# Pooling input and recurrent values as one product with 512 moving columns at a part's start

## The reference

```
proj = h @ w_in[l]
(u_pool, z_ssd, xbc_ssd, dt_ssd, q_h, f_h, i_h, g_h, q_mem, gate_logits) = jnp.split(proj, split_at, axis=-1)
branches = (pool_mixer(u_pool, ...), ssd_mixer(z_ssd, xbc_ssd, dt_ssd, ...),
            hgrn2_mixer(q_h, f_h, i_h, g_h, ...), memory_attention(q_mem, mem, w_mem_kv[l]))
merged = sum over n of sigmoid(gate_logits)[n] * (branches[n] @ w_branch[l, n])
h = layer_norm(ALPHA * h + merged @ w_o[l], ...)
h = layer_norm(ALPHA * h + moe_ffn(h, ...), ...)
```

## Time and profile before

| | |
|---|---|
| median of 3 runs | 2230.35 us (2230.19 to 2231.26) |
| the profiled execution, its own time | 2230.57 us |
| its span | 2228.8 us |
| PE matmuls busy | 2190.8 us, 98% |
| DVE busy | 1180.9 us, 53% |
| ACT busy | 700.2 us, 31% |

### The profile page before, as it was taken

The page is one execution under the profiler, slowest core; times in us unless marked ns, Lnnn a source line. Parts: engine busy times, 40 slices in busy tenths (PEclk is TensorE's granted clock), DMA queues, the critical chain, the costliest instruction groups (busy, mean ns, idle before and its releaser), DMA issues.

```text
span 2228.8 us, 29982 instructions
## 1 busy us (share of the span) xinstructions
PE 2190.8 (98%) x11648; PEld 1535.4 (69%) x11648; DVE 1180.9 (53%) x1495; ACT 700.2 (31%) x778; POOL 12.4 (1%) x28
## 2 busy tenths in 40 slices
PE   8999999999999999999999999999999999999996
PEld 7889899898888888888888944444444444444442
DVE  6457786777765545444557733443333444433435
ACT  4443434444353333344343311111111111111112
POOL 1000000000000000000000000000000000000000
PEclk9999999999999999999999999999999999999998
DMA  7444444444455555555656599999999999999996
GB/s 287 170 176 155 161 151 162 151 162 151 156 185 196 192 195 188 188 193 192 236 209 236 227 383 427 427 427 428 428 428 428 428 428 429 428 429 429 428 427 276
DMA packets 62174, 635.28 MB, mean 285 GB/s; under 512 B 7424, under 2 KB 7552, under 8 KB 10384
## 3 DMA queue, kind: packets, MB, share of 16 engines
q1 hardware_dynamic: 60192, 627.30, 71.1%
q0 software_dynamic: 752, 4.75, 0.6%
q10 hardware_dynamic: 1152, 2.10, 0.3%
HBM read 632.02 MB, written 2.10 MB: 285 GB/s over the span
## 4 chain that ended last, share of the span: by engine, by line
PE 75%; DMA 18%; DVE 5%; issue 1%; ACT 1%; SPq 0%; DVEq 0%; ACTq 0%
PE bank L328 28%; DMA wgu<-wgu 17%; PE bank L893 13%; PE bank L296 8%; PE bank L941 5%; PE bank L281 5%; PE bank L298 4%; PE bank L558 3%; PE bank L841 3%; PE bank L851 3%; DVE wlo L1286 1%; DVE fr L1498 1%; DMA wdt_raw<-wdt 1%; PE bank L874 0%; DMA raw<-units 0%
## 5 line engine op out<-in xcount | busy, mean ns | idle before, releaser
L1286 DVE TENSOR_TENSOR wlo<-raw,whi 128x2048 fp32r<-128x2048 f32 x185 | 423.9, 2291 | 344.7 <-ACT whi L989 344.1
L989 ACT ACTIVATE whi<-raw 128x2048 fp32r<-128x2048 f32 x185 | 354.1, 1914 | 421.6 <-PE bank L328 344.4
L893 PE MATMUL bank<-wgu,xg 128*64 128x512 f32 x2048 | 448.8, 593 | 3.9 <-DMA wgu<-wgu 3.9
L893 PEld LDWEIGHTS bank<-wgu,xg 128*64 128x64 f32 x2048 | 145.5, 137 | 300.4 <-issue 281.9
L296 PE MATMUL bank<-x_split,whi 128*128 128x512 f32 x896 | 319.8, 400 | 0.8 <-DVE wlo L1286 0.8
L328 PE MATMUL bank<-whi,x_split 128*128 128x512 f32 x1024 | 319.6, 390 | 0.0
L298 PE MATMUL bank<-x_split,wlo 128*128 128x256 f32 x896 | 251.1, 280 | 0.0
L941 PE MATMUL bank<-wd,eactT 128*64 128x512 f32 x1024 | 226.8, 596 | 0.0
L328 PEld LDWEIGHTS bank<-whi,x_split 128*128 128x128 f32 x1024 | 192.2, 188 | 39.9
L1832 DVE SCALAR_TENSOR_TENSOR eact<-eth,bank 128x256 f32<-128x256 f32 x32 | 13.5, 422 | 364.6 <-issue 192.7
L328 PE MATMUL bank<-wlo,x_split 128*128 128x512 f32 x512 | 199.4, 389 | 0.0
(11 more groups left out here) (378 smaller groups left out, 2869.2 us busy)
## 6 DMA issues: line engine op xcount, KB each, us to landing
wgu<-wgu SPq DMA_DIRECT2D x128, 2048.0 KB, 21.6
raw<-units SPq DMA_DIRECT2D x204, 1024.0 KB, 4.9
wd<-wd SPq DMA_DIRECT2D x64, 2048.0 KB, 18.7
raw<-units SPq DMA_DIRECT2D x6, 512.0 KB, 6.9
stage<-units SPq DMA_DIRECT2D x2, 1024.0 KB, 13.0
h<-xtok POOLq DMA_DIRECT2D x2, 1024.0 KB, 9.1
out<-acc SPq DMA_DIRECT2D x3, 512.0 KB, 2.6
stage<-units SPq DMA_DIRECT2D x2, 512.0 KB, 9.3
```

What stands on the lines that cost most here:

```text
L893: mi = nc.tensor.matmul(bank[3][CAP * j:CAP * j + CAP, :], buf[:, 4 * c + k, CAP * (2 * half + j):CAP * (2 * half + j + 1)], wgu_t[c][:, j ...
L989: nc.scalar.activation(whi[u % SPLIT][:, :], raw[u % RAW][:, :], ACT.Copy).then_inc(hi_done, 1)
L1286: V.tensor_tensor(wlo[u % SPLIT][:, :], raw[u % RAW][:, :], whi[u % SPLIT][:, :].bitcast(f32), ALU.subtract).then_inc(lo_done, 1)
```

## The change

The inputs POOL and VAL become one, PV, of four units with 4 x 128 rows of 512 columns (256 of pooling, 256 of values), multiplied by `dense_wide` into banks 0 and 1: the left half of each bank is the pooling input, the right half the values. It stands behind QMEM at a part's start, so that PE's program of a part begins with the third and fourth unit of PV, and ends with QMEM and the first two units of PV of the next part. The order is QMEM, PV (4), FGT, QRY, XS, BC, OGATE, ZG. The number of units of a part stays 18. ACT copies the values right behind the pooling input. In the last part the last four places are the first four units of the merge, which goes on with its fifth. HALF_BANK, the banks of the memory values and of the merge change with it.

As unit numbers of the steps from FGT to OGATE rise by two, so do the u at which ACT and DVE do them (5 becomes 7, and so on; ZG stays at 18). The reciprocal of rh and its two products, which stood at u = 21 and 22, are made functions `root_out` and `head_out` and stand at u = 5 and 6 of the next part's loop, behind the last part on their own. The first masks stay at the start of a part's loop, one step later than the join of QMEM.

```diff
-HALVES = 9
-QMEM, POOL, FGT, QRY, XS, BC, OGATE, VAL, ZG = range(HALVES)
-UP = 2 * HALVES
+QMEM, PV, FGT, QRY, XS, BC, OGATE, ZG, NEXT_QMEM, NEXT_PV = range(10)
+FIRST_UNIT = (0, 2, 6, 8, 10, 12, 14, 16, 18, 20)
+UP = 18
...
-HALF_BANK = {QMEM: 0, FGT: 2, QRY: 0, XS: 2, BC: 0, OGATE: 2, ZG: 2, HALVES: 0}
+HALF_BANK = {QMEM: 2, FGT: 2, QRY: 0, XS: 2, BC: 0, OGATE: 2, ZG: 0, NEXT_QMEM: 2}
...
+        for j in range(2):
+            dense_wide(pe, N_P0 + 2 + j, N_P0 + 2 + j, bank[0:2], xhi, xlo, WK * j, j == 0, False)
...
-                n = N_P0 + 2 * h + j
+                n = N_P0 + FIRST_UNIT[h] + j
                 if j == 0:
 
-                    if h == POOL:
-                        pe.wait_ge(s["y1_ok"], p + START)
-                    elif h == VAL:
-                        pe.wait_ge(s["dec_ok"], 3 * p + 3)
-                    elif (h, p) != (FGT, 0):
-                        pe.wait_ge(s["join_ok"], joins(p, {FGT: QMEM, QRY: QMEM, XS: FGT, BC: QRY, OGATE: XS,
-                                                           ZG: OGATE, HALVES: BC}[h]) - (h == FGT))
-                if h == HALVES and last_part:
-                    if j == 0:
+                    if h == QRY:
+                        pe.wait_ge(s["u_ok"], p + 1)
                         pe.wait_ge(s["vh_ok"], p + 1 + START)
-                    dense_wide(pe, p * UP + n, n, bank[0:2], xhi, xlo, WK * j, j == 0, False)
-                elif h in (POOL, VAL):
-                    dense(pe, p * UP + n, n, bank[5], xhi, xlo, UK * j, j == 0, j == 1, True)
+                    else:
+                        pe.wait_ge(s["join_ok"], joins(p, {FGT: QMEM, XS: FGT, BC: QRY, OGATE: XS, ZG: BC,
+                                                           NEXT_QMEM: OGATE, NEXT_PV: ZG}[h]))
+                if h in (NEXT_QMEM, NEXT_PV) and last_part:
+                    i = 2 * (h - NEXT_QMEM) + j
+                    dense_wide(pe, p * UP + n, n, bank[2:4], xhi, xlo, WK * i, i == 0, i == 3)
+                elif h in (PV, NEXT_PV):
+                    dense_wide(pe, p * UP + n, n, bank[0:2], xhi, xlo, WK * j, j == 0, j == 3)
                 else:
...
-            half(1, 0)
-            half(1, 1)
-            half(2, 0)
+            half(PV, 2)
+            half(PV, 3)
+            half(FGT, 0)
...
-            half(7, 0)
+            half(ZG, 0)
             level(6)
-            half(7, 1)
+            half(ZG, 1)
...
-            half(8, 0)
+            half(NEXT_QMEM, 0)
             level(8)
-            half(8, 1)
-            half(HALVES, 0)
+            half(NEXT_QMEM, 1)
+            half(NEXT_PV, 0)
 
...
-                if u == 4:
-                    act.wait_ge(unit_used, half_count(p, 2))
+                if u == 6:
+                    act.wait_ge(unit_used, half_count(p, PV + 1))
                     act.wait_ge(s["dp_ps"], p + START)
-                    nc.scalar.activation(upool[:, :, :], b3(5), ACT.Copy).then_inc(s["u_ok"], 1)
-                if u == 5:
+                    nc.scalar.activation(upool[:, :, :], banks[:, 0:2, 0:UC], ACT.Copy).then_inc(s["u_ok"], 1)
+                    act.wait_ge(s["o_ps"], p + START)
+                    nc.scalar.activation(vh[:, :, :], banks[:, 0:2, UC:2 * UC], ACT.Copy).then_inc(s["vh_ok"], 1)
+                if u == 7:
                     act.wait_ge(s["dp_ps"], p + 1 + START)
                     act.wait_ge(s["yp_ps"], p + START)
                     nc.scalar.activation(dpool[:, :, :], b3(7), ACT.Copy).then_inc(s["dp_ok"], 1)
-                if u == 7:
+                if u == 9:
                     act.wait_ge(s["join_ok"], joins(p, FGT))
...
-                if u == 16:
-                    act.wait_ge(unit_used, half_count(p, 8))
-                    act.wait_ge(s["o_ps"], p + START)
-                    nc.scalar.activation(vh[:, :, :], b3(5), ACT.Copy).then_inc(s["vh_ok"], 1)
...
+            def root_out(q):
+
+                dve.wait_ge(s["osd_ok"], q + 1)
+                step(V.reciprocal(rh, rh))
+
+            def head_out(q):
+
+                step(V.scalar_tensor_tensor(rh, bank[6][:, :], hnw[:, 0:1], rh, ALU.mult, ALU.mult))
+                V.scalar_tensor_tensor(yT[:, 2, bass.ts(q, 2), :], rh.rearrange("p (a b) -> p a b", a=2), 0.5,
+                                       gs[:, :, :], ALU.mult, ALU.mult).then_inc(s["yh_ok"], 1)
...
                     joined(qm[:, :, :], QMEM)
+                if u == 5:
                     dve.wait_ge(s["dec_ps"], 3 * p + START)
                     masks(0)
-                if u == 5:
+                    if p > 0:
+                        root_out(p - 1)
+                if u == 6 and p > 0:
+                    head_out(p - 1)
+                if u == 7:
                     masks(1)
                     if p > 0:
                         state_out(p - 1)
                     dve.wait_ge(s["ys_ok"], 2 * p + START)
...
-                if u == 21:
-
-                    dve.wait_ge(s["osd_ok"], p + 1)
-                    step(V.reciprocal(rh, rh))
-                if u == 22:
-                    step(V.scalar_tensor_tensor(rh, bank[6][:, :], hnw[:, 0:1], rh, ALU.mult, ALU.mult))
-                    V.scalar_tensor_tensor(yT[:, 2, bass.ts(p, 2), :], rh.rearrange("p (a b) -> p a b", a=2), 0.5,
-                                           gs[:, :, :], ALU.mult, ALU.mult).then_inc(s["yh_ok"], 1)
 
             if p == PARTS - 1:
+                root_out(p)
+                head_out(p)
                 state_out(p)
 
         for p in range(PARTS):
```

## The result

The changed kernel takes 2248.16 us (median of 4 runs, 2247.59 to 2248.89), the kernel before 2230.81 us in the same runs: a ratio of 1.0075 [1.0063, 1.0087], **17.4 us slower**. The forecast was 2243.9 in a range of 2238 to 2249, so sign and range held. The time lies 0.2 us above the 2248 to which the forecast's own case went, the clock's 1.5 us included. The sum in it was +13.5, and 3.9 us are missing from it. The profiled execution took 2248.89 us.

The account below looks back on a forecast made before the run. TensorE was taken to bound the parts, so its waits there arrive in full. Boundaries between parts +12.9, last boundary +5.3, wider product -4.7 gave +13.5 us: 2243.9 us, range 2238.0 to 2249.0.

Parts of the forecast that it names:

- the forecast's own case: Waits at all four boundaries, width gain as in the rows: 2239.8 to 2246.4, to 2248 with the clock; chance 0.78.
- the clock's 1.5 us: Extra time if the clock falls in the last boundary's 5.3 us wait, giving 2245.4.
- The bound, TensorE's waits for low halves: In the parts only TensorE's stay moves the end; what is gained or lost there arrives in full.
- The wait at place 1: Second unit after the sums of squares: TensorE waits 3.0 us, as ScalarE's loop head precedes its high half.
- The wait at place 2: Forget gate's first unit: another 1.3 us, as VectorE's masks and reciprocal stand ahead of its low half.
- Seven waits with some 18 us: Expected profile of TensorE's waits for low halves: three of 3.0, three of 1.3, one of 5.3 us.
- The three boundaries together: Boundaries between parts: 4.3 us each by both waits, 12.9 us in all, bounds 9.9 to 14.4.
- The last boundary: Behind the last part: VectorE's reciprocals and products precede place 1's low half; 5.3 us wait (5.0 to 5.6).
- The rival with a falling clock: Clock falls in waits: 1.5 us at the last, up to 6 with all; many waits or no width gain: 0.09.
- The gain from the width: 16 pooling and value units with 512 instead of 256 columns: 0.295 us each, 4.7 us gained (4.0 to 5.5).
- The faster rival: No boundary waits because low halves keep ahead; place 1's high half must start by 242.2: 2225.7 us; chance 0.06.
- Only the last boundary waits: Rival: ScalarE's head falls in idle time and the masks fit, leaving +5.3 - 4.7: 2231.0 us; chance 0.07.

Follow-up runs that it names:

- e1_half_first: Changed kernel with ScalarE's high half for place 1 ahead of its loop's head and VectorE's join of qm behind that unit's low half: 2239.71 us.
- e3_last: Changed kernel with the norms' last steps behind the last part spread over the merge, and ScalarE's first branch copy one step later: 2240.88 us.
- e2_masks: Changed kernel with VectorE's first two masks behind the head products instead of ahead of the reciprocal: median 2248.46 us, profiled execution 2243.71.
- e5_fill: Changed kernel with matmuls nobody reads in TensorE's waits, 12 at each boundary between parts and 20 at the last: 2245.04 us.
- e8_qm_at_head: e4_all with qm's copy and join back at the start of the part: 2228.87 us, ratio 0.9992 to the kernel before.
- e7_all_narrow: e4_all with each 512-column PV matmul made as two of 256: 2231.8 us, ratio 1.0006 to the kernel before.
- e4_all: Changed kernel with the edits of e1_half_first, e2_masks and e3_last together, and qm copied and joined in the part before: 2227.62 us, ratio 0.9984.
- e4_again: The same kernel as e4_all, measured once more beside the kernel before: 2227.24 us, ratio 0.9985.
- e6_narrow: Changed kernel with each 512-column PV matmul made as two of 256 columns: 2250.73 us, ratio 1.0087 to the kernel before.
- after_again: The changed kernel unaltered, measured once more beside e5_fill and others on one chip: 2247.63 us, ratio 1.0073.

## Why the prediction was right, and where the sum was off

- **The bound, TensorE's waits for low halves: right.** The waits that e1_half_first and e3_last took away arrived at the end in full, and a little more; what e2_masks took away did only where the clock held.
- **The wait at place 1, 3.0 forecast: right in cause, half a microsecond short in size.** The list has 3.1, 3.0 and 3.1, but it counts from the end of the last matmul of place 0; counted as the forecast did, from a place 0 of 5.46 us, it is 3.5, 3.4 and 3.4. What made it was shown by e1_half_first. The way from the second root to the high half took 3.8 us and was 3.2 in the sum: the second DMA issue took 0.95 us (0.90 and 0.95 at the next two boundaries) where the earlier trace rows had 0.39. At the third boundary of the kernel before the same issue takes 0.86, so one boundary was read where three stood in the trace. Place 0 to place 1 thus takes 8.92 us where the sum had 8.46.
- **The wait at place 2, 1.3 forecast: right in cause, hidden in the result.** It stands as 1.15 where the clock held (third boundary, e5_fill) and was covered where it fell. "Seven waits with some 18 us" was therefore not what the profile showed: five over a microsecond, with 14.0 + 1.15 = 15.2 us. That VectorE's order makes it is shown by e2_masks and e8_qm_at_head.
- **The three boundaries together: 12.9 forecast, 14.3 measured**, as 16.13 + 15.85 + 15.79 less 3 x 11.15. Nearly all of the 1.4 is the longer head. From the forecast's own 2 x 5.46 it is 15.0, above its upper bound of 14.4.
- **The last boundary: 5.3 forecast, 7.1 measured.** The wait, from the cause given, was 4.8 in the list and 5.2 counted as the forecast did; it cost 4.3, because it took in the wait of 0.4 that the kernel before had at place 3, and the slow clock added 2.7. Here the step failed that kept the clock out of the sum "because no wait inside the trace is long enough to tell". The rival with a falling clock priced it at 1.5 us here, and it is what happened, in both profiled executions of the changed kernel. How much it takes differs from one execution to the next: the 552 matmuls from place 1 on take 128.19 and 127.59 us in the two profiles of the changed kernel, 126.80 in e1_half_first and 127.01 in e2_masks, and 125.41 in e5_fill, whose clock held. That rival's other half, some 4.5 of its 6 us for the three waits of 3.0, did not come: the clock fell at two of three boundaries and cost little there, because the slow matmuls covered the second wait. That the terms overlap was not seen in the prediction, which added them. That the total stayed within the range is owed to the room left for that rival.
- **The gain from the width: 4.7 forecast, 4.2 to 4.9 measured** (e7_all_narrow against e4_all). The Trainium skill, TensorE: Matmul & The Clock Gate, Back-to-back issue gap, would have 1.0 us here by its formula N / 2.4 + 2.5 ns; the runs speak against it, with 0.28 to 0.30 us a unit for its 0.06.
- **The gain seen without the waits is only 3.4 to 3.6** (e4_all, e4_again against before), about a microsecond less than the width is worth. e7_all_narrow against before gives it the same sign, +0.6 in a thousand, but its interval [0.9997, 1.0016] includes 1. In e4_again's profile the two middle periods are 122.67 and 122.66 us, 1.13 and 1.14 under 123.80, which is what four units of 0.28 to 0.30 give; in e4_all's, the same kernel, they are 123.07 and 123.06. So in one execution the new order costs nothing in the middle parts, and in the other 0.4 us a part. What it costs beside the waits on the whole is not settled.
- **The sum again**, with measured terms: 14.3 + 7.0 - 3.5 = +17.8, against +17.4 measured. Against the forecast's terms that is 1.4 more at the parts' boundaries, 1.7 at the last one and 1.2 in the gain, 4.3 where 3.9 were missing; the 0.4 between them are within the scatter of the runs.
- **The faster rival** needed a high half by 242.2; counted from place 0 it started at 4.64 us where 1.06 was wanted, 3.6 late. "Only the last boundary waits" fell by the same trace: ScalarE's 2.85 us of idle time lie ahead of the root, and the head stands behind it.

## What to carry to other kernels

When steps are renumbered to follow a moved product, compare what stands ahead of the first unit behind each loop boundary: a loop's head (its DMA issues and table load) moved by one unit cost three waits of 3 us here, and one conversion put ahead of it gave most of them back with the head unchanged. Read what stands in such a head at every boundary of the trace, not at one: the DMA issue took 0.39 us at the first and 0.86 at the third. Where a forecast contains a wait of several microseconds on TensorE, add to it the slower matmuls behind it, from whatever row of the trace shows that clock; a second wait close behind may be hidden in them, and a small wait that was there before may go into the new one. The gain of a change and its cost in order are separate: here the width's gain was real, and most of it reachable, in the version that put the order right (2227.2 to 2227.6 us).

## What the runs showed of the hardware

- **The granted clock around a wait.** At a wait of 4.8 us it fell to 0.50 (1.2 GHz) in all five profiles that have one with TensorE idle in it: for 6.8 us in both executions of the changed kernel and in e6_narrow, for 3.4 in e1_half_first and e2_masks. In four of the five it fell before the wait was over (0.9 us before in the changed kernel's profile), in e2_masks 0.3 us after. At waits of 3.0 to 3.1 us it fell at two of three boundaries in both executions of the changed kernel, at both in e3_last and at none of three in e2_masks; at e6_narrow's waits of 2.5 and 2.6 it fell at all three; each time for 3.4 us. It even fell once behind a wait of 1.3 us, at the router, in two profiles (after_again at 1274 us, e2_masks at 1268), a wait that the changed kernel's first profile has too without a fall. So the length of the wait alone does not say whether the clock falls. Under half clock a matmul with 512 columns takes 0.43 us instead of 0.23. e2_masks' runs lie 6.4 us apart, which fits a clock that falls in some and not in others, but no other kernel shows it: the changed kernel's runs lie 1.3 and 2.6 apart, those of e4_again, without such waits, 1.3. The Trainium skill, TensorE: Matmul & The Clock Gate, HAM oscillation, has idle gaps send the clock back to half; these rows agree where the clock fell, and e5_fill, whose clock held at all four boundaries with TensorE at work, shows it from the other side.
- **Work that nobody reads can shorten the time.** 20 matmuls in a wait of 4.8 us took 2.7 us off what follows, against one profile of the changed kernel, and 2.1 against the other (138.65 and 138.05 us for the merge's first 576 matmuls, 135.95 with them).
- **A slow stretch can hide a wait.** 16.13 and 15.85 us with it, 15.79 without: it cost 0.1 to 0.3 us at a boundary whose next half was late anyway.
- **A DMA issue on ScalarE's queue** took from 0.34 to 0.95 us at the boundaries. The same instruction took 0.39, 0.39 and 0.86 us at the three boundaries of the kernel before and 0.95, 0.90 and 0.95 after; what makes it longer no run here separates.
